# Expert weights in quads and the memory's key and value weights as row pieces

## What is computed

```
h = silu(x @ w_gate[e]) * (x @ w_up[e])      # 34 x 1024 by 1024 x 2816, twice
y = h @ w_down[e]                            # 34 x 2816 by 2816 x 1024
```

```
m = rmsnorm(mem, g_mem[L])                   # 256 x 1024
k, v = split(m @ w_xkv[L], 2, axis=-1)       # 1024 x 2048
```

## Time and profile before

| what | before |
|---|---|
| median of 3 runs | 2233.07 us (2229.24 to 2236.18) |
| span of the profiled execution | 2237.3 us |
| PE busy in it | 2117.3 us, 95% |
| DVE, ACT busy | 725.7 us, 642.1 us |
| DMA moved | 725.21 MB, mean 324 GB/s |
| granted TensorE clock, mean | 0.995 |

### The profile page before, as it was taken

How to read it: one execution, slowest core, us unless ns; L and a number is a source line. 1 busy time by engine, 2 the same in 40 slices (tenths; PEclk the granted TensorE clock), 3 DMA queues, 4 the chain that set the end, 5 groups by cost and what they waited for, 6 DMA issues and landing times.

```text
span 2237.3 us, 27188 instructions
## 1 busy us (share of the span) xinstructions
PE 2117.3 (95%) x12048; PEld 1298.9 (58%) x12048; DVE 725.7 (32%) x1041; ACT 642.1 (29%) x1024; POOL 42.5 (2%) x73
## 2 busy tenths in 40 slices
PE   9999999999899989999899899989999999999999
PEld 9987443333333333333333333337888998988997
DVE  8983110010010010010010010016665564876553
ACT  6664110010010010010010010005565444965442
POOL 3101000000000000000000000000000000000000
PEclk9999999999999999999999999999999999999999
DMA  7529999999999999999999999997444656544653
GB/s 238 176 96 389 408 403 430 430 425 429 429 426 430 429 426 429 429 425 429 430 424 429 429 426 430 429 422 238 139 169 156 203 188 197 173 158 151 198 189 113
DMA packets 153551, 725.21 MB, mean 324 GB/s; under 512 B 8662, under 2 KB 106378, under 8 KB 127962
## 3 DMA queue, kind: packets, MB, share of 16 engines
q1 hardware_dynamic: 152248, 721.47, 80.7%
q0 software_dynamic: 608, 1.36, 0.2%
q10 hardware_dynamic: 578, 0.64, 0.1%
HBM read 722.38 MB, written 1.07 MB: 323 GB/s over the span
## 4 chain that ended last, share of the span: by engine, by line
PE 59%; DMA 30%; DVE 6%; ACT 3%; issue 1%; SPq 0%; DVEq 0%; ACTq 0%
PE bank L1356 22%; PE bank L1232 17%; DMA weight_ring<-in_w_up_dram 12%; DMA weight_ring<-in_w_gate_dram 9%; DMA weight_ring<-in_w_down_dram 8%; PE bank L1191 5%; PE bank L1314 4%; PE bank L1387 2%; DVE weights_ring L2443 1%; PE bank L1162 1%; PE bank L1048 1%; DVE arena L2503 1%; PE bank L1289 1%; PE bank L1573 1%; PE bank L1596 1%
## 5 line engine op out<-in xcount | busy, mean ns | idle before, releaser
L1232 PE MATMUL bank<-weight_ring,arena 128*64 128x506 f32 x3036 | 644.9, 563 | 34.0 <-DMA weight_ring<-in_w_up_dram 17.8
L1232 PEld LDWEIGHTS bank<-weight_ring,arena 128*64 128x64 f32 x3036 | 213.4, 134 | 425.2 <-issue 384.4
L1314 PE MATMUL bank<-weight_ring,arena 128*64 128x512 f32 x1408 | 323.2, 611 | 64.1 <-DMA weight_ring<-in_w_down_dram 64.1
L2803 DVE SCALAR_TENSOR_TENSOR arena<-arena,bank 128x506 f32<-128x506 f32 (+1 forms) x48 | 28.0, 638 | 913.5 <-ACT arena L2036 913.5
L2835 DVE TENSOR_TENSOR weights_ring<-weight_ring,weights_ring 128x2048 fp32r<-128x2048 f32 x110 | 249.8, 2289 | 126.6 <-ACT weights_ring L2137 126.3
L1314 PEld LDWEIGHTS bank<-weight_ring,arena 128*64 128x64 f32 x1408 | 100.4, 140 | 275.8 <-issue 191.5
L1356 PE MATMUL bank<-input_high,weights_ring 128*128 128x256 f32 x1920 | 248.5, 281 | 0.7 <-issue 0.7
L1356 PEld LDWEIGHTS bank<-input_high,weights_ring 128*128 128x128 f32 x1920 | 234.6, 188 | 3.0 <-issue 2.5
L2137 ACT ACTIVATE weights_ring<-weight_ring 128x2048 fp32r<-128x2048 f32 x109 | 205.6, 1908 | 60.1 <-DMA weight_ring<-in_w_ffn_down_dram 41.0
L1191 PE MATMUL bank<-arena 128*128 128x256 f32 x512 | 142.9, 404 | 0.0
L1191 PEld LDWEIGHTS bank<-arena 128*128 128x128 f32 x512 | 87.3, 189 | 82.6 <-issue 75.6
(11 more groups left out here) (425 smaller groups left out, 1969.6 us busy)
## 6 DMA issues: line engine op xcount, KB each, us to landing
weight_ring<-in_w_down_dram SPq DMA_DIRECT2D x62, 2816.0 KB, 21.7
weight_ring<-in_w_up_dram SPq DMA_DIRECT2D x61, 2816.0 KB, 20.0
weight_ring<-in_w_gate_dram SPq DMA_DIRECT2D x60, 2816.0 KB, 19.3
weight_ring<-in_w_ffn_gu_dram SPq DMA_DIRECT2D x44, 1024.0 KB, 5.1
weight_ring<-in_w_ffn_down_dram SPq DMA_DIRECT2D x22, 1024.0 KB, 4.8
weight_ring<-in_w_in_dram SPq DMA_DIRECT2D x16, 1024.0 KB, 6.3
arena<-in_w_xkv_dram SPq DMA_DIRECT2D x8, 2048.0 KB, 23.4
weight_ring<-in_ab_w_in_dram SPq DMA_DIRECT2D x12, 1024.0 KB, 7.7
```

Source lines behind the costliest of these rows:

```text
L1232: last = pe.matmul(bank[first_bank + c][MPAD * half:MPAD * half + MPAD, 0:(hi - lo) * HF], xs3[:, s, :], rows[:, :, HF * half:HF * half + HF],
L1314: last = pe.matmul(bank[6][MPAD * half:MPAD * half + MPAD, :], hidT[:, at:at + MPAD], W[:, j * D + 512 * half:j * D + 512 * half + 512], s ...
L2803: dve.scalar_tensor_tensor(out=v, in0=v, scalar=1.0, in1=bank[c][:, 0:HF * (hi - lo)], op0=ALU.add, op1=ALU.mult)\
```

## The change

It has two parts.

Keys and values: a load is now a piece of rows. Piece q of layer L holds, for each partition p, the rows 8p + 2q and 8p + 2q + 1 with all 2048 columns, 16 KB in one run. Each piece is used in eight blocks (`kv_block`), four for the keys and four for the values; a block sums over two row tiles only (four matmuls, eight instructions), and DVE adds it to `kT2` or `v2` (`kv_add`), or copies it for the first piece of a layer. There are 64 blocks, four in the gate of each expert from 1 to 14 (after the slots 0, 2, 4, 6) and eight in that of expert 15. Pieces 1 to 7 are issued in the even experts 2 to 14, behind the up loads; piece 0 after expert 0's down loads. For the same order of rows the memory's rows are transposed with a stride, and its gains (`g_mem_2`) come by a GpSimd DMA of their own.

Expert weights: from expert 1 on a load is four slots (`quad_load`, 5632 KB), issued when four slots are used, and PE waits for a landing in front of every fourth slot. The last expert's down weight stays in pairs. In expert 0 slot 4 of the up weight is loaded early into the place that the first piece had (`up_aside`), so that the down weight is loaded in pairs only.

```diff
-    def kv_load(pair):
-        src = t["w_xkv_2"][pair // 4].rearrange("(t p) n -> p t n", p=P)
-        at = 512 * (pair % 4)
-        sp.dma_start(tiles(kvw[:], KT), src[:, :, at:at + 512]).then_inc(S("kv_landed"), 16)
+    def quad_load(name, e, q):
+        sp.dma_start(W[:, 4 * q * DFF:4 * (q + 1) * DFF], rows_of(name, e)[:, 4 * q * DFF:4 * (q + 1) * DFF])\
+          .then_inc(landed(2 * q), 16)
+    def kv_load(piece):
+        L, q = piece // 4, piece % 4
+        src = t["w_xkv_2"][L:L + 1].rearrange("a (p t) n -> p (a t n)", p=P)
+        sp.dma_start(kvw[:], src[:, 4 * D * q:4 * D * (q + 1)]).then_inc(S("kv_landed"), 16)
...
     def rest_of_expert(e):
-        for g in range(PAIRS):
-            sp.wait_ge(S("gate_used"), 8 * e + 2 * g + 2)
-            pair_load("w_up", e, g)
-        if e % 2 and e + 1 < EXP:
-            sp.wait_ge(S("kv_used"), e + 1)
-            kv_load((e + 1) // 2)
+        for q in range(2):
+            sp.wait_ge(S("gate_used"), 8 * e + 4 * q + 4)
+            quad_load("w_up", e, q)
+        if e % 2 == 0:
+            sp.wait_ge(S("kv_used"), kv_blocks_through(e))
+            kv_load(e // 2)
+        if e < EXP - 1:
+            for q in range(2):
+                sp.wait_ge(S("up_used"), 8 * e + 4 * q + 4)
+                quad_load("w_down", e, q)
+            return
...
     sp.wait_ge(S("y_ready"), 2 * H)
-    kv_load(0)
+    slot_load("w_up", AHEAD_SLOT - 1, S("apart_landed"), up_aside)
...
-    sp.wait_ge(S("gate_used"), 5)
-    slot_load("w_up", AHEAD_SLOT - 1, landed(2))
-    sp.wait_ge(S("gate_used"), ESLOTS)
-    slot_load("w_down", AHEAD_SLOT, landed(AHEAD_SLOT))
-    pair_load("w_down", 0, PAIRS - 1)
+    for g in range(PAIRS - 2, PAIRS):
+        sp.wait_ge(S("gate_used"), 2 * g + 2)
+        pair_load("w_down", 0, g)
...
     sp.wait_ge(S("up_used"), AHEAD_SLOT)
-    slot_load("w_down", AHEAD_SLOT - 1, landed(2))
+    kv_load(0)
     for e in range(1, EXP):
-        for g in range(PAIRS):
-            sp.wait_ge(S("down_used"), 8 * e - 8 + 2 * g + 2)
-            pair_load("w_gate", e, g)
+        for q in range(2):
+            sp.wait_ge(S("down_used"), 8 * e - 8 + 4 * q + 4)
+            quad_load("w_gate", e, q)
...
+            pool.dma_start(tiles(mem_gains, 2), t["g_mem_2"].rearrange("l (p t) -> p l t", p=P)).then_inc(S("bias_landed"), 16)
...
+            def kv_block(n):
+                piece, values, c = n // 8, n // 4 % 2, n % 4
+                m3 = tiles(mm[:, 2048 * (piece // 4):2048 * (piece // 4) + 2048], KT)
+                if n % 8 == 0:
+                    pe.wait_ge(S("kv_landed"), 16 * (piece + 1))
+                if n == 0:
+                    pe.wait_ge(S("norm_out"), 8 * 2)
+                else:
+                    pe.wait_ge(S("kv_taken"), n)
+                at = D * values + 256 * c
                 for a in range(2):
+                    for i in range(2):
+                        m = m3[:, 2 * (piece % 4) + i, :]
+                        if values:
+                            w, x = m[:, P * a:P * a + P], kw3[:, i, at:at + 256]
+                        else:
+                            w, x = kw3[:, i, at + P * a:at + P * a + P], m
+                        last = pe.matmul(bank[7][:, 256 * a:256 * a + 256], w, x, start=(i == 0), stop=(i == 1))
+                last.then_inc(S("kv_used"), 1)
...
                     if use == 1 and e:
-                        if s == 0:
-                            pe.wait_ge(S("kv_taken"), e)
-                        kv_step(e, s)
+                        first = kv_blocks_through(e - 1)
+                        if e == EXP - 1:
+                            kv_block(first + s)
+                        elif s % 2 == 0:
+                            kv_block(first + s // 2)
...
-                if e == 0:
-                    pe.wait_ge(S("xs_taken"), 3)
-                    pe.wait_ge(S("norm_out"), 8 * 2)
-                    for i in range(KT):
-                        kv_step(0, i)
...
+            def kv_add(n):
+                at = 2048 * (n // 32) + 512 * (n % 4)
+                dst = (v2 if n // 4 % 2 else kT2)[:, at:at + 512]
+                dve.wait_ge(S("kv_used"), n + 1)
+                if n // 8 % 4 == 0:
+                    ins = dve.tensor_copy(dst, bank[7][:])
+                else:
+                    ins = dve.tensor_tensor(dst, dst, bank[7][:], ALU.add)
+                ins.then_inc(S("kv_taken"), 1)
```

More of the change, by code:

```diff
@@ L66, with kv_blocks_through @@
 VEC_COUNT = [sum(n for _, n in rows) for rows in VEC_ROWS]
+KV_PIECES = 8
+KV_BLOCKS = 8 * KV_PIECES
+def kv_blocks_through(e):
+    return 4 * e if e < EXP - 1 else KV_BLOCKS
 def constants():
@@ L245, in build @@
         mm = z(2 * KT * 256, 8192)
[L246 removed]
+        kvw = z(2 * 2 * D, 12288)
+        up_aside = z(DFF, 12288)
+        mem_gains = VC[:, 192:208]
         utok = z(TT * D, 16384)
@@ L339, in build @@
         A_USES = [len([k for k in range(NA) if k % CSLOTS == s]) for s in range(SLOTS)]
-        B_USES = [(3 * EXP - (s == PAIRS - 1) if s < PAIRS else 1) if s < ESLOTS else 0 for s in range(SLOTS)]
+        B_USES = [((3 * EXP if s % 2 == 0 else 4) - (s >= PAIRS - 2) if s < PAIRS else 1) if s < ESLOTS else 0 for s in range(SLOTS)]
         LAST_ROWS = (FT - 1) * D
@@ L349, in pair_landed @@
         def pair_landed(eng, e, g, use):
-            eng.wait_ge(landed(g), 16 * (A_USES[g] + 3 * e + use - (g == PAIRS - 1)))
+            loads = 3 * e + use if g % 2 == 0 or e == 0 else 4
+            eng.wait_ge(landed(g), 16 * (A_USES[g] + loads - (g >= PAIRS - 2)))
         class Projections:
@@ L515, in _ @@
                 if k == 0:
-                    for name, n in VEC_ROWS[0][7:]:
+                    for name, n in VEC_ROWS[0][6:]:
                         vec_row_load(sp, 0, name, n)
@@ L593, in rest_of_expert, with slot_load @@
                         pair_load("w_down", e, g)
-            def slot_load(name, s, sem):
-                sp.dma_start(expert_slot(s), rows_of(name, 0)[:, s * DFF:(s + 1) * DFF]).then_inc(sem, 16)
+            def slot_load(name, s, sem, home=None):
+                sp.dma_start(expert_slot(s) if home is None else home, rows_of(name, 0)[:, s * DFF:(s + 1) * DFF]).then_inc(sem, 16)
             sp.wait_ge(S("proj_ready"), 2 * last_a_use(0))
@@ L1177, in row_slots @@
                     last.then_inc(S("hidT_ready"), 1)
[L1179 to L1185, removed]
-                for a in range(2):
[L1187 to L1194, removed]
+            def kv_block(n):
[8 more added lines that the diff above has]
+                at = D * values + 256 * c
+                for a in range(2):
+                    for i in range(2):
[6 more added lines that the diff above has]
+                last.then_inc(S("kv_used"), 1)
             def rows_to_features():
@@ L1217, in hidden @@
                         w = ahead[:, n * DFF:(n + 1) * DFF]
-                    elif e == 0 and s == AHEAD_SLOT:
-                        pe.wait_ge(S("apart_landed"), 48)
+                    elif e == 0 and s == AHEAD_SLOT - 1:
+                        pe.wait_ge(S("apart_landed"), 64)
+                        w = up_aside
                     elif e == 0 and s == 1:
                         pe.wait_ge(S("half_landed"), 16)
-                    elif s % 2 == 0:
+                    elif s % (4 if e else 2) == 0 and (e or s != AHEAD_SLOT):
                         pair_landed(pe, e, s // 2, use)
@@ L1302, in _ @@
                     while pairs <= DOWN_SLOT[j] // 2:
-                        pair_landed(pe, e, pairs, 3)
-                        if e == 0 and pairs == PAIRS - 2:
-                            pe.wait_ge(landed(AHEAD_SLOT), 32)
+                        if e in (0, EXP - 1) or pairs % 2 == 0:
+                            pair_landed(pe, e, pairs, 3)
                         pairs += 1
@@ L1741, in _ @@
                .then_inc(S("logit_landed"), 16)
-            for name, n in VEC_ROWS[0][0:7]:
+            for name, n in VEC_ROWS[0][0:6]:
                 vec_row_load(act, 0, name, n)
@@ L2023, in take_slots @@
                 act.activation(chosen, bank[2 if e else 6][:, SLOT_COLS], ACT.Copy).then_inc(S("slots_taken"), 1)
-            def take_kv(u):
-                act.wait_ge(S("kv_used"), u + 1)
-                at = 2048 * (u // 8) + 512 * (u % 4)
-                act.activation((v2 if u // 4 % 2 else kT2)[:, at:at + 512], bank[7][:], ACT.Copy).then_inc(S("kv_taken"), 1)
             for e in range(EXP):
                 exp_tanh_set()
-                if e:
-                    take_kv(e)
                 act.wait_ge(S("gate_used"), 8 * e + 8)
@@ L2796, in scatter_add @@
                     dve.tensor_tensor(rows, rows, bank[6 + n % 2][:], ALU.add).then_inc(S("scatter_taken"), 1)
+            def kv_add(n):
[7 more added lines that the diff above has]
+                ins.then_inc(S("kv_taken"), 1)
             for e in range(EXP):
+                if e:
```

(2 more changed lines are left out.)

22 lines of the change are left out of this document (10 added, 12 removed).

## The result

The changed kernel takes 2359.95 us (median of 4 runs, 2352.26 to 2362.53), the kernel before beside it 2232.11 (4 runs, 2229.24 to 2236.18): a ratio of 1.056, 95% interval 1.0535 to 1.0579. The direction was forecast, the size was not: +50 us were expected, and 2359.95 lies outside the range of 2252 to 2311.

What follows compares the result with a forecast made beforehand. The prediction took DMA, with no free time in the expert stage, as the bound. Start of stage 4.8, experts 2 to 14 29.3, last expert 8.1 and clock 8 made 50 us on 2233: 2283 us, range 2252 to 2311.

Steps and rivals of the forecast that it cites:

- The reserve of two queued pairs: Expert stage before the change: at each issue two pairs are already queued or in flight, hiding every irregularity of the PE.
- TensorE's own timetable: PE work per half in an expert: gate 13.7 us (bounds 13.4 and 14.1), up 10.7, down 9.5.
- The last expert: Expert 15, with eight blocks instead of one unit: 85.7 us against 77.6 before, +8.1.
- For both together I keep 1.1 to 1.8: Each quad load: PE's release to first packet 1.0 us, last packet to PE's start 0.4; together 1.1 to 1.8.
- The rule behind the price: Quad loads: packets move 1.0 us after the PE's release; DMA idles only if the previous quad has landed by then.
- The clock: Lowered TensorE clock after longer waits in 15 experts: 0.5 us per expert, +8 us, bounds 0 to 38.
- rival 3: Expert stage: the clock falls behind every wait and costs the full 38 us: 2313 or a little less; chance 0.17.
- DMA's share: Sign in the expert stage: DMA share 0.97 to 0.98 instead of 1.00, idle time behind gate quad 0.
- Gate starts: Sign in the expert stage: starts of successive experts' gates 83 and 87 us apart in turn.
- Rival 1: Expert stage: quads are free, DMA never idles because the PE is earlier than timed: 2230 to 2240 us; chance 0.07.
- Rival 2: Expert loads: rows of 45 KB raise DMA's rate; faster above 462 GB/s, about 2215 us at 480; chance 0.06.
- Rival 4: The blocks' one bank: each block waits for DVE, 1 us per block, 64 us in all: 2345 us; chance 0.03.

Runs made afterwards that it cites:

- fillers: The changed kernel with small matmuls of ones before gate and up slots and in the down half, 36 per expert: 2344.88 us, ratio 1.050.
- release alone: The changed kernel with loads issued when four slots are used, but as two pair loads, TensorE waiting for each pair separately: 2239.32 us, ratio 1.001.
- up alone: The changed kernel with only the up weights of experts 1 to 15 as quads, gate and down by pairs: 2235.41 us, ratio 1.0005.
- the kv part alone: The changed kernel with its key and value pieces, small blocks and DVE adds, but expert weights loaded in pairs as before: 2231.18 us, ratio 0.999.
- half blocks: The changed kernel with the second row tile of each key and value block left out, output not the reference's: 2343.62 us, ratio 1.048.
- half blocks, fillers: The changed kernel with one row tile of each key and value block left out and 36 small matmuls added per expert: 2319.3 us, ratio 1.036.
- double blocks: The changed kernel, loads still as quads, with each key and value block computed twice: 2468.83 us, ratio 1.103.

## Why the prediction was right in its direction and wrong in its size

**Right.** The reserve of two queued pairs was what the change spent, and DMA's idle time appears with it (share 0.93). TensorE's own timetable held: a gate half at full clock, four slots and two blocks, takes 13.7 us (from 295.5, the end of the first half, to 306.59 + 2.60 = 309.2), as worked out. The issue was followed by the first packet after 0.96 to 0.97 us in all 16 quads of the after kernel that were issued after the previous load had landed; 1.0 was taken. The last expert was forecast at 85.7 us and took 87.2. The kv part, the DVE adds and the moved loads cost nothing.

**The step that failed** is the sentence "For both together I keep 1.1 to 1.8": the start of a load, priced by its 1.0 us before the first packet and 0.4 behind the last. For a quad issued to an idle DMA, landing comes 15.7 us after the issue at the least and 16.5 on average for up quad 0, so it costs 2.3 to 3.1 us beyond the 13.4, plus 0.1 to the PE's start, where the range allowed 1.1 to 1.8 in all. The packets of up quad 0 of expert 1, on each of the 16 DMA engines, show where it is:

```
issue                            295.56
first packets start              296.5 to 297.4   each takes 1.76 to 2.89 us
packets 2 to 8                   298.7 to 309.4   each takes 1.665 us to 1.67
last packet ends                 310.4 to 311.1
landed                           311.45
```

The first packet on an engine takes 0.7 us longer than the others (mean of the 16 loads 2.2 to 2.4 us), the engines are up to 0.7 us apart at the end, and a landing waits for the last. None of this is in an idle time before the first packet. The earlier trace rows had it: 1024 KB is 2.44 us at 430 GB/s and the load took 4.8, so 2.4 are the start. I read the 1.00 us of silence from that row and left out that the 3.4 us behind it ran at 308 GB/s. The Trainium skill, "DMA: Bandwidth & Descriptors", section "Anatomy of one DMA", fits a DMA issued by GpSimd with about 2.0 us plus its bytes at 436 GB/s. That would be 15.2 us for a quad; these loads, issued by SyncE, took 15.7 or more.

These 16 quads, issued after the previous landing, fall in two groups, and the first packet explains only one. Ten land 15.7 to 16.1 us after their issue, six 16.8 to 17.4. In each of the six, and in none of the ten, a packet of 16,384 B of the queue that the page calls `instruction` is moved meanwhile; it takes 0.88 to 0.98 us on one of the 16 engines, and a landing waits for the slowest engine.

**The rule behind the price was too sharp as well.** I let a load come free of charge when it is issued 1 us before the previous one lands. Sorted by that lead (previous landing minus issue, both from the records of the loads), the quads of the changed kernel, those issued right behind a kv piece and the last expert's up quads left out, took this much more than 13.4 us after the later of the two moments:

```
lead, us         loads   extra, us each
below -1          10        3.2
-1 to 1            6        2.5
1 to 2            12        1.7
2 to 3            20        0.8
3 to 4            12        0.4
above 4           18        0.0
```

The extra sums to 89 us, and my rule gives these loads 22 (1.4 each to the first ten, 1.2 to the six, 0.1 to the next twelve). That is 67 of the 77 us by which the forecast was low. Five of an expert's six quads, for which I had almost no idle time, pay 0.4 to 1.0 us each on average, though they are issued 2.5 to 5.7 us ahead.

Part of this is again the `instruction` packets. Of the loads with a lead of 2 to 3 us, the ten in whose time such a packet starts took 1.4 us extra, the other ten 0.3; with 3 to 4 us it is 1.0 and 0.0, above 4 us 0.1 and 0.0. Over the whole table they go with some 26 of the 89 us. The kernel before moves as many of them, and its pair loads, which have over 4 us of lead but for three of 161, pay 0.1 us each on average (0.2 with such a packet). No run took these packets away, so their share rests on this sorting alone.

**The clock** was given 8 us, bounds 0 to 38. Two gate starts of the changed kernel, experts 6 and 8:

```profile
733.90 3.91 PE L1258 MATMUL bank<-weight_ring,arena 128*64 128x506 f32 x12 [2.06 <-DMA weight_ring<-in_w_gate_dram]
...
916.85 2.60 PE L1258 MATMUL bank<-weight_ring,arena 128*64 128x506 f32 x12 [1.15 <-DMA weight_ring<-in_w_gate_dram]
```

The 15 waits are 1.15 to 6.44 us long, 4.0 on average as forecast, and 14 of the 15 first slots are slow, all but that at 916.85; over the 15 they take 1.7 us more than 2.60 each on average. That is what the Trainium skill's rule in "TensorE: Matmul & The Clock Gate", section "HAM oscillation", would have given, 17 us above my sum for the gate starts; the trace agrees with it in 14 of the 15. From landing to the issue of up quad 0 the first gate half took 15.9 us on average in the experts 1 to 14, not 14.1. With fillers it took 14.5. What that is worth in the end is not fully settled: the fillers, which didn't reach every start and take time themselves, gave 15 and 24 us. So the term was low by some 7 at least, and rival 3 (2313, which took this as the whole story) was out: 63 us of the clock's loss removed bought 15.

It enters the path by the issue of up quad 0, in the experts 1 to 14 on average 1.9 us after the previous landing where I had 0.7, which is 16 us, against the 8 that the forecast held. With it the sum closes: 67 + 8 = 75 us, where the stage is 74 longer than forecast. This is a sum made from one trace after the fact, with smaller terms left out (the loads not in the table, the kv pieces some 4 us cheaper than I took them, expert 1's start 3 later), and no experiment set the two terms apart.

**The other forecasts.** DMA's share is 0.90 to 0.96 in the stretches of 100 us from 400 to 1500, not 0.97 to 0.98. Gate starts lie 91.3 us apart on average (1187.4 / 13), not 83 and 87. Rival 1 (quads free) would have been true of release alone, of up alone, and of no kernel with both steps in every half. Rival 2 (faster packets from long rows) is out: a packet of 45,056 B takes 1.665 us and one of 22,528 B 0.84, and two pair loads in a quad's place cost the same. Rival 4 (the bank waits for DVE) is out by the kv part alone.

**Why half blocks gave back so little.** They gave 16 us, and 40 with fillers, where half of 64 blocks' work is 57. The records of the loads, from the landing of expert 1's first gate quad to that of expert 15's last up quad, part the time in two: how long quads were issued after the previous landing, and what they took beyond 13.4 us each from the later of the two moments. The rest of the stretch is the same in all: 87 quads at 13.4 us, and 34 to 36 us of kv pieces.

```
                        stretch, us   issued late   beyond 13.4
changed kernel              1329           32            96
fillers                     1318           15           103
half blocks                 1309            9            99
half blocks, fillers        1289            2            88
double blocks               1439          104           132
```

A shorter gate half, or a faster one, can give back the lateness, of which there were only 32 us. What the starts cost stays: up quad 0 is then issued on average 0.1 us before the previous landing (with fillers 1.4) and still pays 2.3 us (1.8). Added work has no such limit: it makes the loads later, and more of them.

**What stays open.** Why the first packet is slower, and why a load issued 1 to 2 us before the previous landing still pays 1.7 us.

## What to carry to other kernels

Where DMA is the bound, look at how far ahead of the previous landing each load is issued. In this kernel loads were free from 4 us on (from 3, where no `instruction` packet fell into them), and below 2 us they paid 1.7 to 3.2 us each. Count this from the release of a buffer to the landing of its load, and read the price from issue to landing of the nearest small load less its bytes at the full rate, not from the silence before its first packet. Releasing a ring in coarse steps and waiting for it in coarse steps each look harmless alone; together they turned a pipeline into a chain here (1.001 and 1.007 alone, 1.056 together). Then the consumer's added work shows (109 of 115 us), while work taken away gives back only what made the loads late (16 of 57).

## What was not expected of the hardware

A load into an idle DMA moves its first packet on each engine in 2.2 to 2.4 us on average instead of 1.67, for packets of 45,056 B. A packet of 16 KB of the `instruction` queue, 0.96 us on one engine, goes with a landing 0.3 to 1.1 us later where the load has under 4 us of lead. Packets of 45,056 B run no faster than those of half the size (1.665 us against 0.84). TensorE's granted clock averaged 0.96 with up weights as quads at no cost in time, and fillers of 3.4 us ended 2.7 us before a start that was still slow.
